# Third mixer: the reciprocal of the query norms in four quarters for two of the four head pairs

## What is computed

```python
def rms_norm(x, g):
    ms = jnp.mean(jnp.square(xf), axis=-1, keepdims=True)
    return (xf * lax.rsqrt(ms + RMS_EPS) * g).astype(x.dtype)

def gqa_attention(q, k, v, q_gain, k_gain, cos, sin):   # 8 query heads of 64, 2 key heads, 512 tokens
    q = apply_rope(rms_norm(q, q_gain), cos, sin)
    k = apply_rope(rms_norm(k, k_gain), cos, sin)
    ...
    s = jnp.einsum('bkgqd,bskd->bkgqs', qi, k) * scale
    p = jax.nn.softmax(s, axis=-1)
    return jnp.einsum('bkgqs,bskd->bqkgd', p, v)
...
proj = jnp.einsum('bsgk,gkd->bsgd', branches, w_branch[l])
gates = jax.nn.sigmoid(gate_logits + b_gate[l]).reshape(B, S, N_BRANCH, D)
merged = jnp.sum(gates * proj, axis=2)
```

## Time and profile before

| | |
|---|---|
| median of three runs | 2163.7 us (2162.9 to 2167.1) |
| the profiled execution's own time | 2162.4 us |
| its span in the profile | 2160.1 us |
| PE busy | 2107.2 us, 98% of the span |
| DVE busy | 1038.5 us, 48% |
| ACT busy | 744.2 us, 34% |
| POOL busy | 144.7 us, 7% |

### The profile page before, as it was taken

One profiled execution on the slowest core, in us unless ns is written; L12 is line 12 of the kernel. 1 busy time (PEld: TensorE's weight loads), 2 busy tenths in 40 slices (PEclk: granted clock), 3 DMA queues, 4 the chain that ended last, 5 costly groups with the idle time before them and its releaser, 6 DMA issues.

```text
span 2160.1 us, 25108 instructions
## 1 busy us (share of the span) xinstructions
PE 2107.2 (98%) x10263; PEld 1521.5 (70%) x10263; DVE 1038.5 (48%) x1513; ACT 744.2 (34%) x1066; POOL 144.7 (7%) x149
## 2 busy tenths in 40 slices
PE   9999999999999999999999999999999999999997
PEld 7878888888777778888888766777787544444333
DVE  7875434445666554434446666555563312112123
ACT  7773322333455443223234455333333001010012
POOL 0220000001000010000010010251101000000000
PEclk9999999999999999999999999999999999999999
DMA  5233233223221132233234121241245899999996
GB/s 214 78 104 101 86 91 117 95 73 115 69 72 53 62 107 92 75 117 98 74 112 147 43 67 54 57 103 59 78 144 203 360 401 415 420 419 419 420 419 262
DMA packets 86609, 350.80 MB, mean 162 GB/s; under 512 B 9312, under 2 KB 21856, under 8 KB 62176
## 3 DMA queue, kind: packets, MB, share of 16 engines
q1 hardware_dynamic: 82864, 343.00, 43.5%
q0 software_dynamic: 2192, 2.63, 1.0%
q10 hardware_dynamic: 1440, 3.57, 0.4%
HBM read 347.06 MB, written 2.10 MB: 162 GB/s over the span
## 4 chain that ended last, share of the span: by engine, by line
PE 84%; DVE 6%; ACT 4%; DMA 4%; issue 2%; ACTq 0%; POOL 0%; DVEq 0%; POOLq 0%
PE PS L2039 19%; PE PS L2041 19%; PE PS L2040 19%; PE PS L2405 9%; PE PS L2442 4%; DMA SL<-in_wgu_dram 4%; PE PS L2082 2%; PE PS L2389 1%; PE PS L2156 1%; DVE WL L1554 1%; PE PS L2170 1%; PE PS L2180 1%; DVE XC L1621 1%; PE PS L2390 1%; PE PS L2255 1%
## 5 line engine op out<-in xcount | busy, mean ns | idle before, releaser
L2039 PE MATMUL PS<-HH,WH 128*128 128x512 f32 x1392 | 554.7, 399 | 4.0 <-DVE HL L1594 1.2
L2041 PE MATMUL PS<-HH,WL 128*128 128x512 f32 x1392 | 542.6, 390 | 0.0
L2040 PE MATMUL PS<-HL,WH 128*128 128x512 f32 x1392 | 542.1, 389 | 0.0
L1554 DVE TENSOR_TENSOR WL<-RAW,WH 128x1024 fp32r<-128x1024 f32 (+4 forms) x302 | 344.9, 1143 | 288.8 <-ACT WH L1272 288.2
L1272 ACT ACTIVATE WH<-RAW 128x1024 fp32r<-128x1024 f32 (+4 forms) x302 | 286.3, 950 | 306.7 <-PE PS L2041 283.0
L2039 PEld LDWEIGHTS PS<-HH,WH 128*128 128x128 f32 x1392 | 261.3, 188 | 74.0 <-issue 16.7
L2041 PEld LDWEIGHTS PS<-HH,WL 128*128 128x128 f32 x1392 | 261.3, 188 | 56.0
L2040 PEld LDWEIGHTS PS<-HL,WH 128*128 128x128 f32 x1392 | 261.5, 188 | 54.2 <-issue 2.2
L2405 PE MATMUL PS<-SL,XS 128*64 128x512 f32 x960 | 231.4, 597 | 8.3 <-DMA SL<-in_wgu_dram 8.2
L2405 PEld LDWEIGHTS PS<-SL,XS 128*64 128x64 f32 x960 | 71.1, 136 | 127.5 <-issue 123.0
L2039 PE MATMUL PS<-MH,WH 128*128 128x512 f32 x352 | 136.9, 389 | 0.0
(11 more groups left out here) (332 smaller groups left out, 2674.0 us busy)
## 6 DMA issues: line engine op xcount, KB each, us to landing
SL<-in_wgu_dram SPq DMA_DIRECT2D x120, 1024.0 KB, 22.2
SL<-in_wdn_dram SPq DMA_DIRECT2D x54, 1024.0 KB, 23.8
RAW<-in_w_dram SPq DMA_DIRECT2D x46, 512.0 KB, 3.5
RAW<-in_wg_dram SPq DMA_DIRECT2D x44, 512.0 KB, 3.4
RAW<-in_wu_dram SPq DMA_DIRECT2D x44, 512.0 KB, 3.5
RAW<-in_wd_dram SPq DMA_DIRECT2D x32, 384.0 KB, 3.1
RAW<-in_wqkv_dram SPq DMA_DIRECT2D x24, 512.0 KB, 3.5
RAW<-in_wd_dram SPq DMA_DIRECT2D x32, 320.0 KB, 2.9
```

Of the source, the lines that this page charges most:

```text
L1554: e.tensor_tensor(wl, raw, wh.bitcast(F), ALU.subtract).then_inc(*wlo.did("u", u))
L2039: e.matmul(out, wh[:, w], xh, start=k == 0, stop=False)
L2040: e.matmul(out, wh[:, w], xl, start=False, stop=False)
L2041: m = e.matmul(out, wl[:, w], xh, start=False, stop=k == g.total - 1)
```

## The change

For the third and the fourth pair (q2 and q3) the one reciprocal L1797 over 512 columns becomes four over 128 columns. The first stands where the whole one stood, in `rope_b`. The other three are steps of their own, `rope_r`, put in the list behind the next three pieces of gate or branch projection (i = 7, 8 and 9 of the pattern). The multiplication L1799, now in `dve_roped`, stands behind the fourth. Keys, first and second pair keep their form. No other engine gets another instruction, wait or order; every element gets the same arithmetic.

```diff
@@ -658,8 +658,10 @@
         for c in range(1, 4):
             q = rope(f"q{c}", 12 + c, 2)
-            for w in "qqqqbbqbbbqb" if c == 1 else "qqqqbbqbbbbqbb":
+            for i, w in enumerate("qqqqbbqbbbqb" if c == 1 else "qqqqbbqbbbbqbb"):
                 step(q if w == "q" else br)
+                if c > 1 and 7 <= i < 10:
+                    o.add("rope_r", f"q{c}", i - 6)
                 yield
@@ -1547,6 +1549,11 @@
+        def dve_roped(e, name):
+            e.wait_ge(*roped("r", name))
+            e.scalar_tensor_tensor(out=ROPE[name], in0=ROPE[name], scalar=vec("kg" if name == "k" else "qg"),
+                                   in1=ST[:, :], op0=ALU.mult, op1=ALU.mult).then_inc(*roped.did("n", name))
@@ -1794,10 +1801,18 @@
                 elif kind == "rope_b":
                     name, = a
                     e.wait_ge(*root("rope", name))
-                    e.reciprocal(ST[:, :], ST[:, :]).then_inc(*roped.did("r", name))
-                    e.wait_ge(*roped("r", name))
-                    e.scalar_tensor_tensor(out=ROPE[name], in0=ROPE[name], scalar=vec("kg" if name == "k" else "qg"),
-                                           in1=ST[:, :], op0=ALU.mult, op1=ALU.mult).then_inc(*roped.did("n", name))
+                    if name in ("k", "q0", "q1"):
+                        e.reciprocal(ST[:, :], ST[:, :]).then_inc(*roped.did("r", name))
+                        dve_roped(e, name)
+                    else:
+                        e.reciprocal(ST[:, 0:128], ST[:, 0:128]).then_inc(*roped.did("r", name, 0))
+                elif kind == "rope_r":
+                    name, j = a
+                    cols = slice(128 * j, 128 * j + 128)
+                    e.reciprocal(ST[:, cols], ST[:, cols]).then_inc(*roped.did("r", name, j))
+                    if j == 3:
+                        roped.also("r", name)
+                        dve_roped(e, name)
```

## The result

| | before | with the change |
|---|---|---|
| median, runs side by side | 2164.2 us | 2176.7 us (2173.8 to 2178.2) |
| ratio | | 1.0053, 95% interval 1.0041 to 1.0066 |
| span of the profiled execution | 2160.1 us | 2174.7 us |
| DVE busy | 1038.5 us | 1039.3 us |

The account below looks back on a forecast made before the run. PE was taken to bound the kernel, busy 98% of the span with 84% of the chain. Waits of 4.0 and 3.5 us plus 2.0 for the clock gave +9.5 us on 2163.7: 2173.2 us, range 2168.2 to 2177.0.

Parts of the forecast that it names:

- Three waits: PE's waits in third and fourth pair, 1.42, 0.69 and 1.71 us, charged to the long reciprocal: 3.8 us, all gone.
- The chain to the multiplication: DVE, third pair: from the first quarter's start to the multiplication's end, past a full softmax, 10.07 us.
- waits 5.4 and 5.9: New PE waits, in us, before L2228 (the swap matmul) in the third and fourth pair.
- The price of a quarter: DVE reciprocal over 128 columns: about 0.95 us, or 0.87 in a row; bounds 0.84 and 1.0 us.
- Net wait: Delay of PE's score step behind each new wait: +4.0 us in the third pair, +3.5 in the fourth.
- The clock: PE's granted clock falling in the two new waits: 1.0 us each, 2.0 in all.
- The bound of 1.7 us per fall: Most a wait costs on top through PE's clock, from 4 us at mostly 1.2 GHz near the end.
- The lower bound: Least clock cost of a wait, 0: PE's 2.91 us of idle time left the granted clock at 1.00.
- No fall of the clock: Rival: PE's clock never falls in the new waits; +7.5 us, 2171.2 us; chance 0.22.
- Full fall twice: Rival: PE's clock falls fully for both waits; +10.9 us, 2174.6 us; chance 0.11.
- Absorbed later: Rival: the experts' weight stream at the end absorbs PE's delay; no change, 2163.7 us; chance 0.08.
- The intended gain: Rival: fourth quarter and multiplication end before PE reaches L2228, softmax no longer late; -3.8 us, 2159.9 us; chance 0.04.

Follow-up runs that it names:

- the run with quarters in place: The change, but with all four quarters of both pairs in a row where the whole reciprocal stood, multiplication right behind; ratio 1.0000 to the kernel before.
- the filler: The change plus 22 matmuls ahead of PE's wait before each of the two swap matmuls; ratio 1.0031 to the kernel before, 6.7 us.
- the run with the last quarter ahead of the softmax: The change, but last quarter and multiplication one step earlier, ahead of the next score step's softmax; ratio 0.9997 to the kernel before.

## Why the prediction was right, and where it was small

- **What the change removes.** Three waits, 3.8 us: all three are gone in the trace. Right. But no run turned the 3.8 us into a gain; the most that spreading won is 1.2 us.
- **The chain to the multiplication.** 10.07 us forecast, 10.02 measured; waits 5.4 and 5.9 forecast, 5.31 and 5.81 measured. The price of a quarter, a line through 2 and 512 columns, gave 0.95 us, and 0.93 to 0.95 was measured. The fixed cost of an instruction is there (six quarters at a mean of 926 ns and two at 952, 838 for a plain fourth of 3353), and the run with quarters in place shows that it stays hidden. By the rule on small tiles (Trainium skill, VectorE: DVE Perf Modes, section on the TRN2 errata) the trace agrees in kind: many small tiles pay per tile. Here the six instructions more cost 0.75 us of VectorE (7.46 against 6.71), 0.13 us each, more than the 0.06 us estimated from its figure.
- **Net wait.** +4.0 and +3.5, 7.5 us forecast; with the clock held up by the filler the ruler shows 7.1, +4.0 and +3.1. Right. The 0.4 us too many in the fourth pair lie mostly behind the swap matmul: the sum takes 1.13 + 3.67 = 4.80 us from its start to the score step, and with the filler it is 4.50 (1345.35 to 1349.85). Its 1.13 us are only 0.56 to the start of the next matmul when that one needn't wait; neighbours on PE overlap by more there than the 0.17 us given with the profile of before.
- **The clock, the term that was mis-sized.** "I take 1.0 us each, 2.0 in all". The runs show 4.9 us (12.0 less 7.1), about 2.4 a wait. The bound of 1.7 us per fall, from four microseconds near the end, was not a bound: there the low stretch was 3.3 us long (2149.3 to 2152.6 in the trace of before), here it was 6.8 us both times, 2.4 and 1.1 us of it in the wait and 4.4 and 5.7 us after PE had resumed, which at half the rate is 2.2 and 2.9 us. Why it is twice as long here stays open. The lower bound was weak too: the 2.91 us of the second pair that "left the clock alone" did so in the profiled execution, and lowered it in seven of the other eight traces.
- **The range.** Its terms end at +11.3 us, 2175.0; it holds the measured 2176.7 only by the 2 us put on for the spread of the runs. That much is luck. (By its terms the lower end is 2168.3 and not 2168.2.)
- **The rivals.** No fall of the clock: the filler's run is what that rival describes, 6.7 us. Full fall twice, +10.9: the nearest to the measured 11.5; its chance was put too low, and its 1.7 us a fall were still less than the 2.2 and 2.7 measured. On its side stood the rule that the throttled state is the default (Trainium skill, TensorE: Matmul & The Clock Gate, section on what is actually happening); the trace agrees, 0.50 in both waits. Absorbed later: the first expert weights are 13.9 us late, so no. The intended gain: the run with the last quarter ahead of the softmax shows it in small, 1.2 us of the 3.8.

## What to carry to other kernels

Where engines work through one shared list in order, a piece that is moved behind a cheap-looking step is moved behind that step's waits too: ask for the consumer of the last piece, find its place in the other engine's order, and add up everything that now stands between. Cut a long instruction so that its last piece still stands ahead of the next step that waits for a third engine. And price a new wait on TensorE with what the clock does behind it; filler matmuls tell the two apart in one run.

## What was not expected of the hardware

- The clock costs more behind a wait than the wait's length suggests: 5.3 and 5.8 us of idle time were followed by 4.4 and 5.7 us at 0.50, some 2.4 us of lost time each, where the bare net wait was 4.0 and 3.1 us.
- Identical idle times do not act alike: 2.91 us of idle time in the second pair cost no clock in two traces, 1.6 us in six and 3.0 in one. The kernel before ran from 2161.4 to 2168.6 us; its nine executions with a mean granted clock of 0.999 took 2162.5 us on average, its eight with 0.996 took 2166.9. So part of its spread goes with the clock; how much of it is this wait's is not shown.
